# Feed-forward gate and up products by Strassen's scheme, the inner rows kept in DRAM, in a three-layer sequence model on one core

## What is computed

```python
D_FF = 2816
def swiglu(x, w_in, w_out):
    gu = x @ w_in
    gate, up = jnp.split(gu, 2, axis=-1)
    return (jax.nn.silu(gate) * up) @ w_out
...
h = h + swiglu(rms_norm(h, norm_ffn[i]), ffn_w_in[i], ffn_w_out[i])
```

## Time and profile before

| | |
|---|---|
| median of 3 runs | 4012.16 us (4009.47 to 4022.31) |
| profiled execution | 4012.44 us |
| its span | 4010.7 us |
| PE busy | 3746.3 us, 93% |
| PE weight loads | 2950.5 us, 74% |
| DVE / ACT / POOL busy | 1653.1 / 1011.1 / 1328.9 us |
| mean granted TensorE clock | 0.963 of full speed |
| memory traffic | 221.89 MB, 55 GB/s |

### The profile page before, as it was taken

One profiled execution on the slowest core, in us unless ns is written; L12 is line 12 of the kernel. 1 busy time (PEld: TensorE's weight loads), 2 busy tenths in 40 slices (PEclk: granted clock), 3 DMA queues, 4 the chain that ended last, 5 costly groups with the idle time before them and its releaser, 6 DMA issues. The chain is left out here.

```text
span 4010.7 us, 61539 instructions
## 1 busy us (share of the span) xinstructions
PE 3746.3 (93%) x26273; PEld 2950.5 (74%) x26273; DVE 1653.1 (41%) x1829; ACT 1011.1 (25%) x1235; POOL 1328.9 (33%) x989
## 2 busy tenths in 40 slices
PE   7999999999999899988888799999999999977888
PEld 5776788888877567777777577888888778763667
DVE  5664331231334642226576333213223544168552
ACT  4452210000012552334544311100001330141221
POOL 2432233333332133333333222333333323374242
PEclk9999999999999999998898899999999999988999
DMA  2111111111111132322121111111111102100211
GB/s 91 41 43 40 37 47 47 47 47 47 46 57 44 63 132 89 121 79 66 40 76 45 57 60 42 47 47 47 48 47 40 64 33 84 54 1 1 84 42 68
DMA packets 59509, 221.89 MB, mean 55 GB/s; under 512 B 6592, under 2 KB 6976, under 8 KB 58816
## 3 DMA queue, kind: packets, MB, share of 16 engines
q1 hardware_dynamic: 53568, 198.22, 14.5%
q10 hardware_dynamic: 5760, 20.97, 1.3%
HBM read 181.42 MB, written 37.75 MB: 55 GB/s over the span
## 5 line engine op out<-in xcount | busy, mean ns | idle before, releaser
L149 PE MATMUL ps<-xh,whi 128*128 128x512 f32 x4160 | 1325.8, 400 | 58.4 <-DVE xl L370 10.4
L149 PE MATMUL ps<-xl,whi 128*128 128x512 f32 x4160 | 1315.7, 397 | 0.0
L149 PE MATMUL ps<-xh,wlo 128*128 128x512 f32 x4160 | 1314.3, 397 | 0.0
L149 PEld LDWEIGHTS ps<-xh,whi 128*128 128x128 f32 x4160 | 783.0, 189 | 269.9 <-issue 20.3
L149 PEld LDWEIGHTS ps<-xl,whi 128*128 128x128 f32 x4160 | 786.7, 189 | 190.1
L149 PEld LDWEIGHTS ps<-xh,wlo 128*128 128x128 f32 x4160 | 786.3, 189 | 190.0
L116 POOL TENSOR_TENSOR gap<-ones 128x1 f32<-128x1 f32 x258 | 63.4, 246 | 2228.1 <-PE ps L149 2137.1
L119 POOL TENSOR_TENSOR wlo<-wraw,whi 128x1024 fp32r<-128x1024 f32 (+3 forms) x258 | 645.8, 2503 | 21.5
L117 POOL TENSOR_SCALAR whi<-wraw 128x1024 fp32r<-128x1024 f32 (+3 forms) x258 | 289.1, 1120 | 0.0
L636 DVE TENSOR_TENSOR h<-ps,h 128x1024 f32 x56 | 68.6, 1225 | 420.3 <-PE ps L149 420.3
L713 ACT ACTIVATE sq<-sq 128x1024 f32<-128x1024 f32 x44 | 46.7, 1061 | 763.0 <-DVE sq L727 763.0
(11 more groups left out here) (427 smaller groups left out, 3812.5 us busy)
## 6 DMA issues: line engine op xcount, KB each, us to landing
wraw<-w_ffn_in SPq DMA_DIRECT2D x88, 512.0 KB, 3.3
rw_next<-rw_kept SPq DMA_DIRECT2D x40, 512.0 KB, 5.5
wraw<-w_ffn_out SPq DMA_DIRECT2D x32, 512.0 KB, 3.3
rw_kept<-rw_stage SPq DMA_DIRECT2D x24, 512.0 KB, 2.6
rw_kept<-rw_stage ACTq DMA_DIRECT2D x24, 512.0 KB, 2.6
wraw<-w_ple SPq DMA_DIRECT2D x16, 640.0 KB, 3.9
wraw<-w_b_in SPq DMA_DIRECT2D x18, 512.0 KB, 3.3
wraw<-w_hawk_in SPq DMA_DIRECT2D x10, 640.0 KB, 3.9
```

Of the source, the lines that this page charges most:

```text
L149: last = nc.tensor.matmul(acc[:, hf, :], w[:, s, c:c + P], x[:, kt, hf * HALF:(hf + 1) * HALF], start=start and kt == 0 and n == 0, stop=s ...
```

## The change

Instead of a gate block and an up block over all eight k-tiles, inner tiles 1 to 21 are made by the Winograd form of Strassen's scheme. The two-by-two blocks of the weights are (gate, up) by (even, odd k-tiles), those of the activations (even, odd k-tiles) by (first, second half of the tokens). Seven products, each of 4 k-tiles and 512 tokens, give the four result blocks. Inner tile 0 is still made plainly.

- Four sums of raw weight quarters are made by POOL for each pair (`weights`), four sums of activations (T1 to T4) once per layer by DVE (`t_sums`, `t4_sum`). All seven weight operands are then rounded by ACT (`weight_high`) and subtracted by POOL (`low`, 512 columns each); `whi` and `wlo` hold four of them and new tiles `eh`, `el` three.
- The seven sums go to four banks (`acc`). They are combined by ACT (`first_part`) and DVE (`second_part`, `third_part`, `fourth_part`, `up`, `gate`). Gate and silu are done by half (`gate`, `silu`, `gate_rstd`, `hidden`); the norm factor is still read from `tmp.rstd` in SBUF, by every pair.
- The activation operand is now seven blocks of four k-tiles, high and low, so `hh` and `hl` have no room of their own while pairs are made. A finished inner tile is written to DRAM (`store`), and after the last pair all 22 come back through two staging buffers (`load_tile`), are rounded by ACT (`tile_high`) and subtracted by DVE (`tile_low`) into the space of the activation operand, which has 14 places.
- All 22 inner tiles are made before the first output block; the output blocks still go in groups of 8, 8 and 6.
- Semaphores are shared with other stages, and the scratch area for dynamic DMAs is set to 2048.

```diff
+    STREAM += [(f"ffn_in{_l}", 2, 1024, 1024)]
     for _g, _n in enumerate(FFN_GROUPS):
-        STREAM += [(f"ffn_in{_l}{_g}", 2 * _n, 1024, 1024), (f"ffn_out{_l}{_g}", 8, _n * P, _n * P)]
...
+A11, S2_, A12, S3_, S1_, A22, S4_ = range(7)
+B11, T2_, B21, T3_, T1_, T4_, B22 = range(7)
+PAIR = 7
...
+        xh, xl = (sb(n, [P, PAIR, KD // 2, HALF], F32R) for n in ("ffn_xh", "ffn_xl"))
+        eh, el = (sb(n, [P, 3, HALF], F32R) for n in ("ffn_wh", "ffn_wl"))
+        wsum = sb("ffn_wsum", [P, 2, HALF])
+        part = sb("ffn_part", [P, 4, HALF])
+        stage = sb("ffn_stage", [P, 2, T])
...
+        whole = {A11: (eh, el, 0), S2_: (eh, el, 1), S4_: (eh, el, 2)}
+        shared = {A12: (0, 0), S3_: (0, HALF), S1_: (1, 0), A22: (1, HALF)}
...
+        acc = {n: g.ps[:, 4 + n % 4, :] for n in range(PAIR)}
...
+                sp.wait_ge(g.w_split.sem, first + 2)
+                load_raw(1)
...
+                raw_used(last_pair, 1)
+                load_blocks(sp, g, k_out[0], 0)
+                load_tile(0)
+                load_tile(1)
+                store(last_pair - 1)
+                for i in range(2, 8):
+                    load_tile(i)
+                store(last_pair)
+                for i in range(8, FFN_SLOTS):
+                    load_tile(i)
+                stream_phase(sp, None, nc, g, k_out[0])
+                for i in range(FFN_SLOTS, KF):
+                    load_tile(i)
+                stream_phase(sp, None, nc, g, k_out[1])
...
+                def weights(m):
+                    pool.wait_ge(g.quarters_loaded[1].sem, m * 16 + g.quarters_loaded[1].base)
+                    pool.wait_ge(g.weight_low.sem, m * PAIR + (g.weight_low.base - PAIR))
+                    add(raw[S1_], a21, raw[A22], ALU.add)
+                    pool.wait_ge(g.quarters_loaded[0].sem, m * 16 + g.quarters_loaded[0].base)
+                    pool.wait_ge(g.weight_sum.sem, m * 4 + (g.weight_sum.base - 3))
+                    add(raw[S2_], raw[S1_], raw[A11], ALU.subtract)
+                    low(m, A11)
+                    low(m, S2_)
+                    pool.wait_ge(g.weight_low.sem, m * PAIR + (g.weight_low.base - PAIR + S2_ + 1))
+                    add(raw[S4_], raw[A12], raw[S2_], ALU.subtract)
+                    add(raw[S3_], raw[A11], a21, ALU.subtract)
+                    for n in (A12, S3_, S1_, A22, S4_):
+                        low(m, n)
...
+                with pool.Fori(1, last_pair + 1) as m:
+                    weights(m)
...
+                def pair(m, ready):
+                    pe.wait_ge(g.fourth_part.sem, m + (g.fourth_part.base - 1))
+                    combined(m, A11, acc[A11])
+                    pe.wait_ge(g.up_part.sem, m * 2 + g.up_part.base)
+                    combined(m, S2_, acc[S2_], ready.get(T2_))
+                    pe.wait_ge(g.gate_sum.sem, m * 2 + g.gate_sum.base)
+                    combined(m, A12, acc[A12])
+                    pe.wait_ge(g.third_part.sem, m + (g.third_part.base - 1))
+                    combined(m, S3_, acc[S3_], ready.get(T3_))
+                    pe.wait_ge(g.first_part.sem, m + g.first_part.base)
+                    combined(m, S1_, acc[S1_], ready.get(T1_))
+                    pe.wait_ge(g.second_part.sem, m + g.second_part.base)
+                    combined(m, A22, acc[A22], ready.get(T4_))
+                    pe.wait_ge(g.gate_sum.sem, m * 2 + (g.gate_sum.base + 1))
+                    combined(m, S4_, acc[S4_])
...
+                pair(1, {T2_: 0, T3_: 4, T1_: 8, T4_: 12})
+                with pe.Fori(2, last_pair + 1) as m:
+                    pair(m, {})
+                for grp, fo in enumerate(first_out):
+                    def wait_block(q, s):
+                        pe.wait_ge(g.w_split.sem, q * 2 + (fo + s + 1))
+                        pe.wait_ge(g.acc_free.sem, q * 2 + (fo + s - 1))
+                    wait_block(0, 0)
+                    out_block(grp, 0, kt_ready=True, acc=banks(g, 0))
+                    wait_block(0, 1)
...
+                for i in (0, 1, 2):
+                    row_scaled(i)
+                weight_high(1, A11, first_free)
+                weight_high(1, S2_, first_free)
+                act.wait_ge(g.bc_done.sem, g.bc_done.base + 1)
+                nc.scalar.activation(tmp.rstd, flat(banks(g, 6)), ACT.Copy).then_inc(g.rstd_ready.sem, 1)
+                row_scaled(3)
+                for i in range(KD // 2):
+                    act.wait_ge(g.t_raw.sem, g.t_raw.base + i + 1)
+                    t_high(T2_, i)
+                weight_high(1, A12, first_free)
+                weight_high(1, S3_, first_free)
+                for n in (T3_, T1_):
+                    for i in range(KD // 2):
+                        t_high(n, i)
+                act.wait_ge(g.gate_part.sem, g.gate_part.base + 2)
+                nc.scalar.activation(sg, sg, ACT.Silu).then_inc(g.silu_ready.sem, 2)
+                weight_high(1, S1_, first_free)
+                weight_high(1, A22, first_free)
+                weight_high(1, S4_, first_free)
+                for i in range(KD // 2):
+                    act.wait_ge(g.t_raw.sem, g.t_raw.base + KD // 2 + i + 1)
+                    t_high(T4_, i)
+                with act.Fori(1, last_pair) as m:
+                    free = lambda n: act.wait_ge(g.product_done.sem, prods(m, n))
+                    first_part(m)
+                    weight_high(m, A11, free, 1)
+                    weight_high(m, S2_, free, 1)
+                    weight_high(m, A12, free, 1)
+                    silu(m, 0)
+                    weight_high(m, S3_, free, 1)
+                    weight_high(m, S1_, free, 1)
+                    weight_high(m, A22, free, 1)
+                    silu(m, 1)
+                    weight_high(m, S4_, free, 1)
+                first_part(last_pair)
+                tile_high(0)
+                tile_high(1)
+                silu(last_pair, 0)
+                for i in range(2, 8):
+                    tile_high(i)
+                silu(last_pair, 1)
+                for i in range(8, KF):
+                    tile_high(i)
+                squares_act(act, nc, g, first_out[-1], tmp.sq)
...
+                def t_sums(i):
+                    lower, upper = slice(0, HALF), slice(HALF, T)
+                    dve.wait_ge(g.row_scaled.sem, g.row_scaled.base + i + 1)
+                    ch.link(dve, gained(t_raw[T1_][i], 2 * i, upper, scaled[i][:, lower]))
+                    gained(t_raw[T2_][i], 2 * i + 1, upper, t_raw[T1_][i])
+                    gained(t_raw[T3_][i], 2 * i + 1, upper, scaled[i][:, upper]).then_inc(g.t_raw.sem, 1)
...
+                for i in range(KD // 2):
+                    t_sums(i)
+                for n in (T2_, T3_, T1_):
+                    for i in range(KD // 2):
+                        t_low(n, i)
                 dve.wait_ge(g.rstd_ready.sem, g.rstd_ready.base + 1)
-                for n, before, k_in, k_out, first, first_out, last in groups():
-                    with dve.Fori(0, n) as m:
...
+                dve.wait_ge(g.t_low.sem, g.t_low.base + 12)
+                dve.sem_inc(g.gate_sum.sem, 2)
+                dve.sem_inc(g.up_part.sem, 2)
+                dve.wait_ge(g.block_done.sem, first + 1)
+                nc.vector.tensor_tensor(sg, flat(banks(g, 0)), tmp.rstd, ALU.mult).then_inc(g.gate_part.sem, 2)
+                for i in range(KD // 2):
+                    t4_sum(i)
+                dve.wait_ge(g.silu_ready.sem, g.silu_ready.base + 2)
+                nc.vector.tensor_tensor(sg, sg, tmp.rstd, ALU.mult).then_inc(g.gate_done.sem, 2)
+                dve.wait_ge(g.gate_done.sem, g.gate_done.base + 2)
+                dve.wait_ge(g.block_done.sem, first + 2)
+                nc.vector.tensor_tensor(hid, flat(banks(g, 2)), sg, ALU.mult).then_inc(g.half_ready.sem, 2)
+                for i in range(KD // 2):
+                    t_low(T4_, i)
+                dve.wait_ge(g.half_ready.sem, g.half_ready.base + 2)
+                dve.sem_inc(g.acc_free.sem, 2)
+                with dve.Fori(1, last_pair) as m:
+                    second_part(m)
+                    gate(m, 0)
+                    third_part(m)
+                    gate_rstd(m, 0)
+                    up(m, 1)
+                    fourth_part(m)
+                    up(m, 0)
+                    hidden(m, 0)
+                    gate(m, 1)
+                    gate_rstd(m, 1)
+                    hidden(m, 1)
+                m = last_pair
+                second_part(m)
+                tile_low(0)
+                gate(m, 0)
+                tile_low(1)
+                third_part(m)
+                gate_rstd(m, 0)
+                tile_low(2)
+                up(m, 1)
+                fourth_part(m)
+                tile_low(3)
+                up(m, 0)
+                tile_low(4)
+                hidden(m, 0)
+                tile_low(5)
+                tile_low(6)
+                tile_low(7)
+                gate(m, 1)
```

(7 more changed lines are left out.)

353 lines of the change are left out of this document (276 added, 77 removed).

## The result

| us | before | after |
|---|---|---|
| median (lowest to highest) of the runs side by side | 4010.81 (4007.45 to 4022.31) | 3960.85 (3951.59 to 3965.58) |
| feed-forward stage, layer 0, first matmul to the filler behind it | 741.8 | 714.5 |
| the same, layer 1 | 742.5 | 712.1 |

The ratio of the medians is 0.9868, with a 95% interval of 0.9839 to 0.9896: 50 us faster, where 62 were forecast. The profiled execution is the slowest of the four, 3965.6 us. From it, the page: busy time by engine, the groups of the products, the issues of the new transfers.

A forecast was written before the change was run, and what follows sets the result against it. PE (TensorE) was taken as the bound, busy 93% of the span. The terms -117.6 + 2 x 13.5 + 2 x 14.3 = -62.0 us gave 3950 us; forecast 3930 to 3965 (0.60), eight in ten 3915 to 3982.

The forecast's parts named there:

- lead-in: Behind plain pair 0, DVE making operand sums, met by POOL, holds PE 12.0 us and the clock falls: 13.5 us per layer.
- way through DRAM: Inner tiles stored and reloaded: PE waits 12.8 us after two output blocks, plus 1.5 for the clock: 14.3 us per layer.
- What goes: In 21 pairs of each of 2 layers, 84 matmuls replace 96: 504 fewer at 0.2333 us, 117.6 us saved.
- rival (d): Matmuls come slower with twelve in one bank or two opening waits: 4068 us, or about 4010 at half; chance 0.06.
- Steady pairs at nothing: In combined pairs of 19.6 us, PE stays the bound; DVE's 15 and POOL's 19.5 us loop fit, costing nothing.
- Rival (b): POOL's loop bounds the pairs at 20.5 us, each 0.9 longer: 3970 to 3988 us; chance 0.13 for 3965 to 4000.
- Rival (c): Slower than before through costlier POOL instructions: pair from 21.4 us; at 23 us, about 4030 in all; chance 0.05.

The follow-up runs named there:

- e3: Changed kernel, with SP loading block pair 1's weights ahead of inner tiles 8 to 13 and DVE adding output blocks 0 and 1 to h earlier: 3918.6 us.
- e12: Kernel before the change, with a 32-byte pad ahead of the feed-forward rows xh, xl and 256 bytes more ahead of hh, hl: 3966.9 us, ratio 0.9876.
- e4: Changed kernel, with unused 32-byte strips ahead of whi and behind wlo: 3922.7 us, ratio 0.9773.
- e9: Changed kernel, with two more 128x512 sums that nobody reads on POOL in pairs 2 to 20 of each layer: 4017.1 us, one run.
- e10: Changed kernel, with four more 128x512 sums that nobody reads on POOL in pairs 2 to 20 of each layer: 4095.5 us, one run.
- e8: Changed kernel, with POOL's sums and remainders in pair 1 of each layer cut to 16 of 512 columns: 3939.8 us, one run.
- e1: Changed kernel, with only SP's order changed: block pair 1's weights are loaded ahead of inner tiles 8 to 13: 3967.6 us, one run.

## Why the prediction was right, and where it was off

| per layer, us | forecast | measured, layer 0 | layer 1 |
|---|---|---|---|
| 21 pairs | -58.8 | -63.6 | -63.6 |
| lead-in | +13.5 | +14.8 | +14.2 |
| way through DRAM | +14.3 | +21.5 | +19.0 |
| stage | -31.0 | -27.3 | -30.4 |

(The lead-in is the 15.5 and 15.6 us from above less the 0.7 and 1.4 that the kernel before loses in its first pair. The way through DRAM is what is left of the stage; its waits are 18.3 and 16.8 us.)

**The stages** together are 57.7 us shorter, forecast 62.0. The whole fell by 50.0. The 8 us between lie outside the changed stages. In the two profiled runs it is 11 us, 8 of them behind the second stage, a part that takes 865 to 872 us in the kernels with the old stage and 870 to 875 in the others; so a few microseconds there may be the change's doing, and no run settles it. In e3 the two stages fell by 94.0 and the whole by 94.4, so no larger cost outside them is shown. That the time came within 11 us of the 3950 forecast is in part luck, since errors of the terms cancel over the two layers: the pairs gave 9.6 us more than forecast, the way through DRAM took 11.9 more and the lead-in 2.0.

**What goes**: right in kind, short in size. I read in the earlier trace rows one pace for all matmuls and kept it for operands in new tensors. 36 of a pair's 84 matmuls came 0.0065 us faster, 4.9 us a layer. This was luck of the allocator, not the scheme. Between two kernels at 0.2267, e12 and e4, the change is worth 21.9 and 21.5 us a stage, and padding alone would have brought the old kernel to 3966.9, 6 us from the changed one. One bank for twelve matmuls cost nothing, as the earlier trace rows had it; rival (d) is out.

**Steady pairs at nothing**: right, by a hair. POOL's loop was forecast at 19.5 with the reload and is 18.5 to 19.0 (e9, e10). DVE was to have 15 us and has 11.8, with fewer meetings than the six assumed; POOL 15.1 instead of 16.5. Rival (b) failed by 0.3 to 0.9 us a pair. Rival (c) is what e9 and e10 built: 4017 us at a pair of 20.9 to 21.2, 4095 at 23.0. Its sum in the forecast was wrong: for a pair of 23 us it has about 4030, but 42 pairs at 3.4 us more than 19.6 are 143 us on top of 3950, 4093, less what the loop's lead hides at the start.

**The lead-in**: right in what bounds it. A22 was forecast 51.2 us behind the stage's first matmul (500.9 against 449.7) and started at 51.3 and, in layer 1, 52.2. PE was held for less than the 12.0 us forecast, 10.3 and 9.1, since matmuls at a lower clock filled part of the time; while DVE's chain sets the end, that is no cost of its own. Behind A22 the clock took 2.3 and 1.5 us, where 1.5 was forecast. What was forecast wrongly is the form: two waits on DVE of about 6 us, where there are three, of 2.2, 1.7 and 4.5, one of them for ACT's first part; and from the earlier trace rows I took one fall behind one wait, for a stretch with two falls in layer 0 and three in layer 1. DVE's prices held (0.75 alone, 1.64 met), and e8 showed that the meetings are its greater part.

**The way through DRAM**: the term that was mis-sized. Up to hidden(1) the count was nearly right, 34.0 us behind the last pair's start against 32.6 forecast; PE waited 0.9 us for tile 7, where none was forecast. Two steps behind it failed. The store and two loads were issued within a microsecond and the loads took 5.4 and 6.2 us to land, so ACT had tile 8 at 39.9 instead of about 37; and the weights of block pair 1, issued at 927.78 right behind tile 13's load and beside the weights' second block, landed at 933.79, 6.0 us instead of some 4. I took the landing times of the earlier trace rows, which are those of transfers that go alone; the range had a microsecond more for it. So PE was held there for 17.4 and 15.8 us instead of 12.8. The clock behind the wait cost 2.6 us in layer 0 and, as forecast, 1.5 in layer 1. The forecast had both queues end 1.3 us apart; they end 2.7 apart, and e1 to e3 confirmed that either alone holds PE.

## What to carry to other kernels

When a wait has two releasers that end together, removing one shows nothing; remove both before giving either up. An engine's idle time is room only if its loop isn't closed by a transfer: measure the room by adding work, two doses, and extrapolate to none. And before a product is made cheaper by another scheme, look at the pace of its matmuls against where its two operands start in SBUF: here two unused strips, of 32 and 256 bytes, were worth 20.8 us a stage, nearly as much as Strassen's saving of an eighth with all its costs, 21.9.
